# A two-block transformer kernel: when GpSimd sums squares and makes modulation products, and how the first FFN gets its input

## The chip, the cores and the metric

The kernel runs on one core of one Trainium2 chip. The metric is the device time of one launch in microseconds (us). Five engines have instruction streams of their own: TensorE (PE in the profile, with its weight loads as PEld), VectorE (DVE), ScalarE (ACT), GpSimd (POOL) and SyncE (SP), which here only starts DMAs.

## The reference, cut to what matters

Two transformer blocks are applied to x, 512 tokens by 1024 features, in float32. The part of the first block that this case is about, with `mod` a vector of 6 x 1024 modulation values computed from c:

```python
mod = silu(c) @ w_ada + b_ada
sh1, sc1, gt1, sh2, sc2, gt2 = split(mod, 6)
...
x = x + gt1 * (concat(y_a, y_b, y_c) @ w_out)
h = rmsnorm(x, g_ffn) * (1 + sc2) + sh2
gate, up = split(h @ w_gate_up, 2)             # 1024 -> 2 x 2816
x = x + gt2 * ((silu(gate) * up) @ w_down)     # 2816 -> 1024
```

`rmsnorm(x, g)` divides each token by the root of the mean of its 1024 squares plus 1e-6. After it come a final norm and a second block with two more FFNs of the same size.

## The kernel before, in words

**Layout.** Features lie on the 128 partitions and the 512 tokens along the free dimension. x is 8 tiles of 128x512 (`KD` = 8), an FFN's hidden layer 22 such tiles (`KF` = 22). A float32 product is made from three matmuls (`three`, lines 489 to 491): each operand is split into a high part, rounded to the type fp32r by a copy on ScalarE, and a low part, the difference, by a subtraction on VectorE. high x high, high x low and low x high are summed in one PSUM bank.

**Slabs.** Weights come in slabs of 8 tiles (128x1024, 512 KB), one slab for each output tile of 128 features. Slab s uses buffer s % 2 of `w_raw`, `w_hi` and `w_lo`. SyncE loads it once the low part of slab s - 2 is made. `split_high(s)` (line 997, ScalarE, recorded at L1003) waits for the load and for `w_used` of slab s - 2, that is until TensorE is through with that buffer. `split_low(s)` (line 1400, VectorE, recorded at L1404) then makes the low part and counts up `w_ready`, which TensorE awaits. Slabs 20 to 27 are w_out. Slab 28 is the gate slab of pair 0 of the first FFN, 29 its up slab, 30 and 31 those of pair 1, and so on to 71. A pair is one gate slab and one up slab, 24 matmuls each, and gives one hidden tile.

**Order.** Each engine has its own hand-written instruction stream, and semaphores tie them together. `plan` fixes which PSUM bank each product uses and whose reading frees it.

**From the output projection to the FFN.** For each of the 8 output tiles VectorE adds gt1 times the PSUM bank to x (`add_gated`, L1512), ScalarE squares the new tile into `sq` (L1147, two buffers by turns), and GpSimd adds the square to `acc` (`sums("out1", None)`, L1899). When all 8 are in, TensorE sums `acc` over the partitions in `token_sums` (4 matmuls with one column each, recorded as 8 at L692). ScalarE takes the root (`root`, L1180), VectorE the reciprocal (`token_scale`, L1537), and TensorE spreads the 512 reciprocals over all partitions into a PSUM bank (`spread`, L701, again recorded as 8).

**h.** For each tile k VectorE multiplies x by that bank into `x_scaled` (L1552). ScalarE makes from it `h_full` and `h_hi` by one activation each (L1189), both with the factor `scale2` and the shift sh2 for each feature, and VectorE makes `h_lo` = `h_full` - `h_hi` (`low`, L1410). `x_scaled` and `h_full` have two buffers. TensorE waits for `h_lo` of tile k before the three matmuls with it.

**The first FFN.** TensorE's `pair(0)` runs all of gate slab 28 and then all of up slab 29. ScalarE's `pair(n)` is: high part of slab 2n + 1 of the FFN, silu of the gate bank (L1201), high part of slab 2n + 2, then `hid_hi` (L1209). VectorE's is: low part of slab 2n + 1, low part of slab 2n + 2, `t_hid` = up bank times silu (L1572), then `hid_lo` (L1576).

**GpSimd's products.** The six parts of `mod` are computed in the gaps. GpSimd's share for a part j is `mod_products(j)`: for 8 blocks of w_ada (128x1024, loaded on its own DMA queue by `mod_row` into `sq`) a multiplication by c (L1820 or L1822) and an addition into `acc` (L1824). gt2's follow right behind the square sums and the reading of `acc` by TensorE. TensorE reads them in `mod_columns` after the last gate and up pair. `acc` and `sq` are the same memory for squares and products. The next use of `acc` is `sums("down0", ...)`, in the down projection.

Of the kernel before, what the change touches and what calls it, by code (L numbers as in the profile page):

```python
# [25 lines left out]
P = 128  # L26
T = 512
# [96 lines left out]
def program(nc, ins, out):  # L124
    ctx = ExitStack()
    with ctx:
# [75 lines left out]
        (x_scaled, h_full), _ = region(OVER + 3 * T * BYTES, BIG, [(n, [P, 2, T], F32) for n in ("x_scaled", "h_full")])  # L202
# [268 lines left out]
        def _(pe):  # L471
# [233 lines left out]
            token_sums("ffn0", "out1")  # L705
            spread(("scale", "ffn0"), 4, 1)

            def ffn(f, between):
# [21 lines left out]
                pair(0)  # L730
# [252 lines left out]
        def _(act):  # L983
# [197 lines left out]

            root("ffn0")
            act.wait_ge(mod_set, 2)
            for k in range(KD):
                act.wait_ge(scaled_x, k + 1)
                if k >= 2:
                    act.wait_ge(h_ready, 8 * GEN["ffn0"] + k - 1)
                for dst, done_ in ((h_full[:, k % 2, :], h_whole), (h_hi[:, k, :], h_high)):
                    act.activation(dst, x_scaled[:, k % 2, :], ACT.Identity, bias=modc[:, SH2 + k:SH2 + k + 1],  # L1189
                                   scale=scale2[:, k:k + 1]).then_inc(done_, 1)  # L1190

            def ffn(f, between, down, last=False):
                s0 = S_GU[f]

                def pair(n, i=None):
                    split_high(s0 + 2 * n + 1, i, 2)
# [136 lines left out]
        def _(dve):  # L1333
# [210 lines left out]

            token_scale("ffn0")
            b = wait_filled(dve, ("scale", "ffn0"))
            dve.wait_ge(mod_set, 2)
            for k in range(KD + 1):
                if k < KD:
                    if k >= 2:  # L1550
                        dve.wait_ge(h_high, 8 * GEN["ffn0"] + k - 1)
                    dve.tensor_tensor(x_scaled[:, k % 2, :], x[:, k, :], psum[:, b, :], ALU.mult).then_inc(scaled_x, 1)  # L1552
                if k:
                    j = k - 1
                    dve.wait_ge(h_whole, j + 1)
                    low(h_lo[:, j, :], h_full[:, j % 2, :], h_hi[:, j, :], 8 * GEN["ffn0"] + j)

            def ffn(f, between, before_down, down, last=False):
                s0 = S_GU[f]

                def pair(n, i=None):
                    split_low(s0 + 2 * n + 1, i, 2)
# [233 lines left out]
        def _(pool):  # L1796
# [89 lines left out]
            def sums(phase, clear, kinds=1):  # L1886

                if clear:
                    wait_filled(pool, ("sum", clear))
                    done(pool.memset(acc[:, 0:kinds, :], 0.0))  # L1890
                else:
                    pool.memset(acc[:, 0:kinds, :], 0.0).then_inc(summed, SUM0)
                    pool.wait_ge(summed, SUM0)
# [9 lines left out]
            sums("out1", None)  # L1903
            mod_row(GT2 // KD, 0)
            wait_filled(pool, ("sum", "ffn0"))
            mod_products(GT2 // KD)
            wait_filled(pool, ("mod", GT2 // KD))
            sums("down0", "ffn0", 2)
# [55 lines left out]
```

## Time and profile before

| what | value |
|---|---|
| median of 3 timed runs | 1907.98 us (1907.70 to 1912.42) |
| span of the profiled execution | 1908.4 us |
| mean granted TensorE clock | 0.978 |
| busy: TensorE, weight loads | 96%, 75% |
| busy: VectorE, ScalarE, GpSimd | 50%, 35%, 15% |
| DMA traffic | 181.54 MB, mean 95 GB/s |

The page gives no time of the profiled execution beyond its span from the first to the last instruction; it lies 0.4 us from the median. The busy share of TensorE comes from modelled ends of its matmuls, so two matmuls that follow each other overlap in the records; the distance of their starts is what one costs.

### The profile page before, as it was taken

What the parts mean: (1) busy time and instruction counts of PE and PEld (TensorE: products, weight loads), DVE (VectorE), ACT (ScalarE), POOL (GpSimd) and SP (SyncE); (2) the same over time, 40 slices, a digit from 0 to 9 for tenths busy, and PEclk for the clock granted to TensorE, in tenths of its full rate; (3) what the DMA queues carried; (4) which work ended last, traced back from release to release, by engine and by line L of the source; (5) the groups of instructions that cost most, each with busy time, mean ns of one, the idle gap of its engine ahead of it and who ended that gap; (6) DMA issues with size and microseconds to landing.
All of it is one profiled execution on the core that took longest, in us unless ns stands there. A gap on an engine that the chain in (4) does not pass through costs nothing.

```text
span 1908.4 us, 23358 instructions
## 1 busy us (share of the span) xinstructions
PE 1822.8 (96%) x8239; PEld 1435.6 (75%) x8239; DVE 950.1 (50%) x1401; ACT 663.2 (35%) x1048; POOL 290.9 (15%) x208
## 2 busy tenths in 40 slices
PE   5699989699999999999999999999999999999998
PEld 2567667488888887888888887766678888888886
DVE  5689883643333333444434436776655544444322
ACT  2345563322222323222222223554444332222222
POOL 6287511710000111000001010002100100000000
PEclk9799999699999999999999999999999999999999
DMA  9343202433334232333343342112123333333332
GB/s 343 102 137 106 78 23 66 125 96 99 99 89 115 78 98 72 99 94 93 99 120 91 87 102 72 39 54 63 53 73 96 96 88 99 99 95 96 106 93 73
DMA packets 298399, 181.54 MB, mean 95 GB/s; under 512 B 14636, under 2 KB 285416, under 8 KB 298280
## 3 DMA queue, kind: packets, MB, share of 16 engines
q1 hardware_dynamic: 290336, 157.30, 28.1%
q0 software_dynamic: 6352, 22.26, 3.9%
q10 hardware_dynamic: 1656, 1.25, 0.2%
q8 instruction: 34, 0.56, 0.1%
q14 instruction: 21, 0.17, 0.0%
HBM read 178.69 MB, written 3.09 MB: 95 GB/s over the span
## 4 chain that ended last, share of the span: by engine, by line
PE 79%; issue 5%; DVE 2%; POOL 1%; ACT 0%; POOLq 0%; DVEq 0%; ACTq 0%
PE psum L489 25%; PE psum L491 25%; PE psum L490 24%; PE psum L809 3%; PE psum L817 1%; DVE h_lo L1410 1%; POOL acc L1899 1%; PE psum L701 0%; DVE w_lo L1404 0%; PE psum L692 0%; PE psum L780 0%; DVE x_scaled L1552 0%; PE psum L880 0%; DVE o_tok L1791 0%; PE psum L558 0%
## 5 line engine op out<-in xcount | busy, mean ns | idle before, releaser
L489 PE MATMUL psum<-h_hi,w_hi 128*128 128x512 f32 x1480 | 594.0, 401 | 20.1 <-DVE h_lo L1410 11.0
L490 PE MATMUL psum<-h_lo,w_hi 128*128 128x512 f32 x1480 | 580.0, 392 | 0.0
L491 PE MATMUL psum<-h_hi,w_lo 128*128 128x512 f32 x1480 | 580.0, 392 | 0.0
L1404 DVE TENSOR_TENSOR w_lo<-w_raw,w_hi 128x1024 fp32r<-128x1024 f32 (+1 forms) x258 | 366.9, 1422 | 315.9 <-ACT w_hi L1003 312.3
L489 PEld LDWEIGHTS psum<-h_hi,w_hi 128*128 128x128 f32 x1480 | 279.5, 189 | 144.7 <-issue 65.1
L1003 ACT ACTIVATE w_hi<-w_raw 128x1024 fp32r<-128x1024 f32 (+1 forms) x258 | 286.0, 1108 | 154.1 <-PE psum L491 154.0
L491 PEld LDWEIGHTS psum<-h_hi,w_lo 128*128 128x128 f32 x1480 | 279.8, 189 | 59.9
L490 PEld LDWEIGHTS psum<-h_lo,w_hi 128*128 128x128 f32 x1480 | 280.1, 189 | 55.0 <-issue 0.7
L491 PE MATMUL psum<-hid_hi,w_lo 128*128 128x512 f32 x528 | 210.7, 399 | 0.0
L490 PE MATMUL psum<-hid_lo,w_hi 128*128 128x512 f32 x528 | 208.1, 394 | 0.0
L489 PE MATMUL psum<-hid_hi,w_hi 128*128 128x512 f32 x528 | 207.1, 392 | 0.0
L1899 POOL TENSOR_TENSOR acc<-acc,sq 128x512 f32<-128x512 f32 x48 | 66.0, 1374 | 807.7 <-ACT sq L1147 806.8
L1209 ACT ACTIVATE hid_hi<-t_hid 128x512 f32 (+1 forms) x66 | 41.9, 635 | 284.3 <-DVE t_hid L1572 284.3
L490 PEld LDWEIGHTS psum<-hid_lo,w_hi 128*128 128x128 f32 x528 | 99.1, 188 | 25.7
L489 PEld LDWEIGHTS psum<-hid_hi,w_hi 128*128 128x128 f32 x528 | 99.1, 188 | 23.7
L1572 DVE TENSOR_TENSOR t_hid<-psum,t_silu 128x512 f32<-128x512 f32 x66 | 45.7, 692 | 143.0 <-PE psum L491 143.0
L491 PEld LDWEIGHTS psum<-hid_hi,w_lo 128*128 128x128 f32 x528 | 99.1, 188 | 22.8
L1205 ACT ACTIVATE t_silu<-t_gate 128x512 f32<-128x512 f32 x44 | 27.8, 632 | 160.2 <-DVE t_gate L1567 160.2
L1576 DVE TENSOR_TENSOR hid_lo<-t_hid,hid_hi 128x512 f32 (+1 forms) x66 | 46.9, 711 | 64.8 <-ACT hid_hi L1209 64.8
L1824 POOL TENSOR_TENSOR acc<-acc,sq 128x1024 f32<-128x1024 f32 x28 | 75.6, 2700 | 2.2
L1293 ACT ACTIVATE p<-p,stat 128x512 f32<-128x512 f32 (+2 forms) x64 | 41.3, 645 | 83.5 <-DVE stat L1702 43.8
L1120 ACT ACTIVATE p<-p,stat 128x512 f32<-128x512 f32 x64 | 45.8, 717 | 62.2 <-DVE stat L1463 62.2
(247 smaller groups left out, 1936.1 us busy)
## 6 DMA issues: line engine op xcount, KB each, us to landing
w_raw<-in_w_in SPq DMA_DIRECT2D x50, 512.0 KB, 3.8
w_raw<-in_w_gate_up SPq DMA_DIRECT2D x44, 512.0 KB, 3.8
w_raw<-in_ffn_w_gate SPq DMA_DIRECT2D x44, 512.0 KB, 3.9
w_raw<-in_ffn_w_up SPq DMA_DIRECT2D x44, 512.0 KB, 3.8
w_raw<-in_ffn_w_down SPq DMA_DIRECT2D x32, 704.0 KB, 4.5
sq<-in_w_ada POOLq DMA_DIRECT2D x32, 512.0 KB, 4.2
w_raw<-in_w_down SPq DMA_DIRECT2D x16, 704.0 KB, 4.5
ada_w<-in_w_ada SPq DMA_DIRECT2D x4, 2048.0 KB, 20.8
```

Of the source, the lines that this page charges most:

```text
L489: pe.matmul(o, a_hi, b_hi, start=start, stop=False)
L490: pe.matmul(o, a_hi, b_lo, start=False, stop=False)
L491: return pe.matmul(o, a_lo, b_hi, start=False, stop=stop)
L809: pe.matmul(psum[:, b, 0:P * len(kts)], q_, k_, start=True, stop=True).then_inc(filled[b], 1)
L1003: act.activation(w_hi[:, s % 2, 0:n], w_raw[:, s % 2, 0:n], ACT.Identity).then_inc(w_high, 1)
L1120: act.activation(p1[:, t % 3, m, :], p1[:, t % 3, m, :], ACT.Exp, bias=stat[:, t % 3, m:m + 1], scale=-1.0, accum_out=stat[:, t % 3, 2 + m ...
L1209: act.activation(hid_hi[:, slot_of(n, i), :], t_hid[:, :], ACT.Identity).then_inc(hid_high, 1)
L1404: dve.tensor_tensor(w_lo[:, s % 2, 0:n], w_raw[:, s % 2, 0:n], w_hi[:, s % 2, 0:n].bitcast(F32), ALU.subtract).then_inc(w_ready, 1)
L1572: dve.tensor_tensor(t_hid[:, :], psum[:, b, :], t_silu[:, :], ALU.mult).then_inc(hid_set, 1)
L1576: dve.tensor_tensor(hid_lo[:, at, :], t_hid[:, :], hid_hi[:, at, :].bitcast(F32), ALU.subtract)\
L1824: last = pool.tensor_tensor(mod_acc, mod_acc, ada_row[:, k % 2, :], ALU.add)
L1899: pool.tensor_tensor(acc[:, m, :], acc[:, m, :], sq[:, n, m, :], ALU.add).then_inc(summed, 1)
```

## The change

In the stretch between the output projection and the first FFN:

- GpSimd sums only the squares of tiles 0 to 6. TensorE takes the token sums in two groups of 4 matmuls, the first from `acc`, the second directly from the last square, both into the same bank.
- GpSimd's products for gt2 start when two hidden tiles of the first FFN are ready (`hid_ready` 2), no longer right behind the square sums.
- `x_scaled` is made by one VectorE instruction with `scale2` as its factor for each feature and has four buffers. `h_full` is gone: ScalarE makes only `h_hi` (shift alone), and VectorE makes `h_lo` from `x_scaled`, the shift and `h_hi` in one instruction.
- Both parts of slab 29 are split before the root and the reciprocal on ScalarE and VectorE.
- TensorE runs the first gate and up slab of the first FFN together, tile by tile: for each k three matmuls of gate, then three of up.

```diff
@@ memory
-        (x_scaled, h_full), _ = region(OVER + 3 * T * BYTES, BIG, [(n, [P, 2, T], F32) for n in ("x_scaled", "h_full")])
+        (x_scaled,), _ = region(OVER + 3 * T * BYTES, BIG, [("x_scaled", [P, 4, T], F32)])
@@ TensorE
-            token_sums("ffn0", "out1")
+            b = take(("sum", "ffn0"))
+            for part_, ready in ((acc[:, 0, :], (summed, SUM0 + KD - 1)), (sq[:, 1, 0, :], (squared, KD))):
+                pe.wait_ge(*ready)
+                for i in range(TT):
+                    last = pe.matmul(psum[:, b, i:i + 1], part_[:, P * i:P * i + P], mean_d,
+                                     start=ready[0] is summed and i == 0, stop=ready[0] is squared, skip_group_check=True)
+            last.then_inc(filled[b], 1)
             spread(("scale", "ffn0"), 4, 1)
...
-                pair(0)
+                def first_pair():
+                    for n, key in enumerate(("gate", "up")):
+                        await_slab(s0 + n)
+                        take((key, 0, 0))
+                    for k in range(KD):
+                        pe.wait_ge(h_ready, h0 + k + 1)
+                        for n, key in enumerate(("gate", "up")):
+                            last = three(psum[:, bank_of((key, 0, 0)), :], *tile(s0 + n, k), *hs[k], k == 0, k == KD - 1)
+                            if k == KD - 1:
+                                last.then_inc(w_used, 1)
+
+                if f == 0:
+                    first_pair()
+                else:
+                    pair(0)
@@ ScalarE
+            split_high(S_GU[0] + 1)
             root("ffn0")
             act.wait_ge(mod_set, 2)
             for k in range(KD):
                 act.wait_ge(scaled_x, k + 1)
-                if k >= 2:
-                    act.wait_ge(h_ready, 8 * GEN["ffn0"] + k - 1)
-                for dst, done_ in ((h_full[:, k % 2, :], h_whole), (h_hi[:, k, :], h_high)):
-                    act.activation(dst, x_scaled[:, k % 2, :], ACT.Identity, bias=modc[:, SH2 + k:SH2 + k + 1],
-                                   scale=scale2[:, k:k + 1]).then_inc(done_, 1)
+                act.activation(h_hi[:, k, :], x_scaled[:, k % 4, :], ACT.Identity, bias=modc[:, SH2 + k:SH2 + k + 1])\
+                   .then_inc(h_high, 1)
...
-                    split_high(s0 + 2 * n + 1, i, 2)
+                    if f or n:
+                        split_high(s0 + 2 * n + 1, i, 2)
@@ VectorE
+            split_low(S_GU[0] + 1)
             token_scale("ffn0")
+            dve.wait_ge(mod_set, 2)
             b = wait_filled(dve, ("scale", "ffn0"))
-            dve.wait_ge(mod_set, 2)
             for k in range(KD + 1):
                 if k < KD:
-                    if k >= 2:
-                        dve.wait_ge(h_high, 8 * GEN["ffn0"] + k - 1)
-                    dve.tensor_tensor(x_scaled[:, k % 2, :], x[:, k, :], psum[:, b, :], ALU.mult).then_inc(scaled_x, 1)
+                    if k >= 4:
+                        dve.wait_ge(h_ready, 8 * GEN["ffn0"] + k - 3)
+                    dve.scalar_tensor_tensor(out=x_scaled[:, k % 4, :], in0=x[:, k, :], scalar=scale2[:, k:k + 1],
+                                             in1=psum[:, b, :], op0=ALU.mult, op1=ALU.mult).then_inc(scaled_x, 1)
                 if k:
                     j = k - 1
-                    dve.wait_ge(h_whole, j + 1)
-                    low(h_lo[:, j, :], h_full[:, j % 2, :], h_hi[:, j, :], 8 * GEN["ffn0"] + j)
+                    dve.wait_ge(scaled_x, j + 1)
+                    dve.wait_ge(h_high, 8 * GEN["ffn0"] + j + 1)
+                    dve.scalar_tensor_tensor(out=h_lo[:, j, :], in0=x_scaled[:, j % 4, :],
+                                             scalar=modc[:, SH2 + j:SH2 + j + 1], in1=h_hi[:, j, :].bitcast(F32),
+                                             op0=ALU.add, op1=ALU.subtract).then_inc(h_ready, 1)
...
-                    split_low(s0 + 2 * n + 1, i, 2)
+                    if f or n:
+                        split_low(s0 + 2 * n + 1, i, 2)
@@ GpSimd (in sums, the branch without clear)
-                    pool.memset(acc[:, 0:kinds, :], 0.0).then_inc(summed, SUM0)
-                    pool.wait_ge(summed, SUM0)
+                    pool.memset(acc[:, 0:kinds, :], 0.0).then_inc(summed, 1)
+                    pool.wait_ge(summed, SUM0 + SQUARES[phase])
...
-            sums("out1", None)
+            pool.memset(acc[:, 0, :], 0.0).then_inc(summed, SUM0)
+            pool.wait_ge(summed, SUM0)
+            for n in range(KD - 1):
+                pool.wait_ge(squared, n + 1)
+                pool.tensor_tensor(acc[:, 0, :], acc[:, 0, :], sq[:, n % 2, 0, :], ALU.add).then_inc(summed, 1)
+                pool.wait_ge(summed, SUM0 + n + 1)
+            pool.wait_ge(hid_ready, 2)
             mod_row(GT2 // KD, 0)
-            wait_filled(pool, ("sum", "ffn0"))
             mod_products(GT2 // KD)
             wait_filled(pool, ("mod", GT2 // KD))
-            sums("down0", "ffn0", 2)
+            sums("down0", None, 2)
```

## Rows read from the trace of the kernel before

**Rows 1.** The page, part 1: busy time, share of the span, instructions

```profile
PE 1822.8 (96%) x8239; PEld 1435.6 (75%) x8239; DVE 950.1 (50%) x1401; ACT 663.2 (35%) x1048; POOL 290.9 (15%) x208
```

**Rows 2.** Timeline of TensorE: start us, us, engine, line, operation, count [idle before <-releaser]

```profile
344.20 1.87 PE L692 MATMUL psum<-small,acc 128*128 128x1 f32 x8 [3.08 <-POOL acc L1899]
346.63 2.08 PE L701 MATMUL psum<-ident,rcol 128*128 128x128 f32 x8 [0.57 <-DVE rcol L1537]
351.99 0.77 PE L489 MATMUL psum<-h_hi,w_hi 128*128 128x512 f32 x1 [3.28 <-DVE h_lo L1410]
...
374.26 0.80 PE L489 MATMUL psum<-h_hi,w_hi 128*128 128x512 f32 x1 [1.65 <-DVE w_lo L1404]
...
388.01 0.50 PE L489 MATMUL psum<-h_hi,w_hi 128*128 128x512 f32 x1 [0.94 <-DVE w_lo L1404]
```

**Rows 3.** The chain that ended last, single matmuls: start us, us, what

```profile
375.05 0.43 PE psum L490
...
378.65 0.23 PE psum L491
```

**Rows 4.** Stretches: length, busy us of PE, PEld, DVE, ACT, POOL, PEclk, DMA share, GB/s

```profile
306.00:308.00 2.00, 0.72 (x4) 0.26 (x2) 1.46 (x2) 0.44 (x1) 0.86 (x1) 1.00 0.00 0
...
343.00:344.00 1.00, 0.00 (x0) 0.00 (x0) 0.00 (x0) 0.00 (x0) 1.00 (x1) 0.80 0.15 43
...
368.00:372.00 4.00, 2.69 (x6) 1.66 (x6) 4.00 (x3) 1.71 (x2) 3.91 (x3) 0.50 0.42 131
...
377.00:378.00 1.00, 1.00 (x4) 0.83 (x3) 0.04 (x1) 0.00 (x0) 1.00 (x1) 0.64 1.03 311
```

**Rows 5.** Timeline of ScalarE from the last square on

```profile
342.18 0.63 ACT L1147 ACTIVATE sq<-x_res 128x512 f32 x1 [3.78 <-DVE x_res L1512]
...
349.53 0.81 ACT L1189 ACTIVATE h_full<-x_scaled,modc,scale 128x512 f32<-128x512 f32 x1 [3.16 <-DVE x_scaled L1552]
...
372.64 0.60 ACT L1201 ACTIVATE t_silu<-psum 128x512 f32<-128x512 f32 x1 [2.92 <-PE psum L491]
373.14 1.05 ACT L1003 ACTIVATE w_hi<-w_raw 128x1024 fp32r<-128x1024 f32 x1
```

**Rows 6.** Timeline of VectorE: y stage, scale, first FFN pair

```profile
299.49 0.75 DVE L1495 SCALAR_TENSOR_TENSOR k<-o,sub,psum 128x512 f32<-128x512 f32 x1 [0.27 <-PE psum L664]
300.15 0.69 DVE L1410 TENSOR_TENSOR h_lo<-k,h_hi 128x512 fp32r<-128x512 f32 x1
300.76 0.74 DVE L1495 SCALAR_TENSOR_TENSOR k<-o,sub,psum 128x512 f32<-128x512 f32 x1
...
348.74 1.28 DVE L1552 TENSOR_TENSOR x_scaled<-x_res,psum 128x512 f32<-128x512 f32 x2 [2.17 <-PE psum L701]
...
381.73 0.69 DVE L1572 TENSOR_TENSOR t_hid<-psum,t_silu 128x512 f32<-128x512 f32 x1 [4.70 <-PE psum L491]
383.20 1.92 DVE L1576 TENSOR_TENSOR hid_lo<-t_hid,hid_hi 128x512 fp32r<-128x512 f32 x1 [0.77 <-ACT hid_hi L1209]
385.04 2.91 DVE L1404 TENSOR_TENSOR w_lo<-w_raw,w_hi 128x1024 fp32r<-128x1024 f32 x1
```

**Rows 7.** The line that subtracts for h_lo: durations ns min/median/max

```profile
L1410 DVE TENSOR_TENSOR h_lo<-h_full,h_hi x8: 693/2264/2881, 351.1 to 368.0; 128x512 fp32r<-128x512 f32 x8
```

**Rows 8.** Timeline of GpSimd: last square sum, first and last product

```profile
342.88 1.26 POOL L1899 TENSOR_TENSOR acc<-acc,sq 128x512 f32<-128x512 f32 x1 [4.05 <-ACT sq L1147]
...
348.90 1.89 POOL L1820 TENSOR_TENSOR acc<-sq,cact 128x1024 f32<-128x1024 f32 x1 [2.00 <-DMA sq<-in_w_ada]
...
386.95 3.26 POOL L1824 TENSOR_TENSOR acc<-acc,sq 128x1024 f32<-128x1024 f32 x1
```

**Rows 9.** Groups by line: kinds of row nearest to the new operations

```profile
L1404 DVE TENSOR_TENSOR w_lo<-w_raw,w_hi 128x1024 fp32r<-128x1024 f32 (+1 forms) x40 | 49.8, 1246 | 67.5 <-ACT w_hi L1003 66.4
...
L1158 ACT ACTIVATE h_hi<-x_res,vcol x12 | 8.7, 724 | 68.3 <-DVE x_res L1627 48.3 <-DVE x_res L1778 20.0
...
L1521 DVE SCALAR_TENSOR_TENSOR h_lo<-x_res,vcol,h_hi x14 | 10.5, 752 | 15.4 <-ACT h_hi L1158 15.4
```

## The prediction, made before the changed kernel ran

> **What bounds the kernel now.** I read the page first. TensorE is busy 96% of the span and no other engine over half of it [rows 1], so only time in which TensorE waits or runs slowly can be gained. The 40 slices put such time ahead of about 400 us. The timeline of TensorE then shows the stretch of this change. Its last out-projection matmul ends at about 341.1 (344.20 less 3.08 of idling). The token sums start at 344.20, the spread at 346.63, the first FFN matmul at 351.99, the up slab only at 374.26, and up slab 31 waits until 388.01 [rows 2]. When TensorE doesn't wait, one matmul follows the next after 0.43 us at the lower clock and 0.23 us (24 in 5.44 us) at the higher one [rows 3]. The stretches tell which clock it was: the granted clock halves (2.4 to 1.2 GHz) at about 343.6, some 2.5 us after TensorE went idle, stays at 0.50 through the whole gate slab, where TensorE is busy 2.7 of 4 us, and is back at full at about 377.7, after some 3.4 us of matmuls without a wait [rows 4]. The gate slab took 20.6 us (351.99 until silu, which its end releases, at 372.64 [rows 5]). At full clock it would be 5.44 us.
>
> Why it took so long is in VectorE's and GpSimd's rows. A subtraction of two SBUF tiles, 128x512, takes 0.69 us in the y stage [rows 6], but the eight of `h_lo` have a median of 2.26 and a maximum of 2.88 us [rows 7]. In just this stretch GpSimd runs its products, 348.90 to 390.21 [rows 8]. `x_scaled`, which reads one operand from PSUM, is not drawn out beside them: two in 1.28 us [rows 6]. So VectorE's instructions with two SBUF tiles share something with GpSimd, and they pace TensorE.
>
> **The change, part by part** (times in us on the profiled execution's axis).
>
> **Square sums in two groups.** Now: square done at 342.81 [rows 5], GpSimd's addition 1.26 us [rows 8], token sums from 344.20 to 346.07 [rows 2]. The first group has its input early and runs at about 341.2 behind the last matmul. The second can start at 342.85; if it costs as much as all of today's (1.87 at the lower clock) it ends at 344.7, and the root would let VectorE go on at 345.0. But slab 29's split now stands in front: high part on ScalarE right behind the square, 342.72 plus 1.05 [rows 5], low part on VectorE from 343.8 for 1.25 to 1.45 us (1.25 is the mean of 40 in the FFN [rows 9]). The reciprocal therefore comes at about 345.2. Behind it as now 0.2 us for itself and 2.08 for the spread [rows 2]: `x_scaled` starts at 347.5 where it is 348.74 [rows 6]. **Gain 1.2**. Bounds: 0.8 (a w_lo of 1.5 and a slower second group) and 2.3 (the clock hasn't fallen yet, and the spread takes half). The split itself costs nothing, as until here both engines wait; without that cover it would be 2.3 us, as now after `h`.
>
> **h from x.** To the first `h_lo` now 3.25 us: `x_scaled`, two activations, subtraction [rows 2, 5, 6]. After: an instruction of the kind with a PSUM operand 0.75 [rows 6], one activation with one column of factors or shifts 0.72, a scalar_tensor_tensor of two SBUF tiles 0.75 [rows 9], and 0.25 for three handovers: 2.5 us, first matmul at 350.0. **Gain 0.75**. From then VectorE makes one `h_lo` every 1.33 us: 0.66 from start to start after the kind with PSUM [rows 6], and by its length some 0.67 for the other. ScalarE needs 0.7 for each and isn't the bound. The last is ready at about 359.2.
>
> Here a rule speaks against the change. The rows have the new kind, 0.752 us for 128x512 with x and `h_hi` both in SBUF [rows 9], next to 0.69 for the plain subtraction. The Trainium skill, Vector Engine (DVE) Microarchitecture Reference, section 7 (Points that are easy to get wrong), says that a scalar_tensor_tensor with two SBUF sources that aren't bf16 runs at half throughput. By it one `h_lo` would cost about 1.4 us and the pace be 2.0; by the row the sum stays as it is. I take the row.
>
> **Gate and up together.** TensorE has 48 matmuls, six for each tile: 2.56 us at the lower clock, 1.36 at the higher. Both are more than 1.33, so once started it doesn't wait. The clock is low at 350.0, as TensorE did only small work for 9 us. It rose 3.4 us after the last wait before 377.7 [rows 2, 4]; I take 3.4 to 6.8 and 5.1 as the middle: 12 matmuls slow, 36 at 0.227 = 8.2, up slab done at 363.3 (now 381.7). From start to end that is 13.3 us where it is 29.7. **Gain 16.4**. Bounds: 15.5 and 18.8 (clock high throughout).
>
> **A new wait.** Slab 30 needs slab 28's buffer. Until now that was split under up slab 29; now both buffers come free together. Gate's last matmul ends 0.7 us before up's, at 362.6. Then silu 0.50 to the next start, high part 1.05 [rows 5], low part 1.25 to 1.4: gate slab 30 starts at 365.65 instead of right behind slab 29. **Loss 2.4**. Behind that chain on VectorE is `t_hid`, on ScalarE `hid_hi` and the high part of 31: 0.7 + 0.7 + 1.05 + 1.4 and a `hid_lo` beside it bring slab 31 by 369.6, before slab 30 is through at 371.1. So today's wait of 1.1 us in front of slab 31 (slab 30 is through at 381.5 + 5.44 = 386.9, slab 31 starts at 388.01 [rows 2]) goes. **Gain 1.1**. Slab 31 then starts at 371.1 where it is 388.0: 16.9 so far (the terms add to 17.0).
>
> **The products, later.** They cost the same 41.3 us of GpSimd [rows 8], now from some 2.5 us (the load) after the second hidden tile, over 3 to 4 pairs of 10.9 us. Their result is awaited only after all 22 pairs, some 200 us later; their 8 loads of 512 KB (4 MB in 41 us, 100 GB/s) come beside the kernel's mean of 95 GB/s, where the first slices of the page moved 343. What they do to VectorE is in the rows: in the pair under them `t_hid` at 381.73, `hid_lo` 1.92 us, w_lo 2.91 us, TensorE at 388.01 [rows 2, 6]. That chain, 6.3 us after the up slab, is longer than the 5.44 of the gate slab beside it, hence a wait of 0.94. If only one of the two is drawn out (1.23 or 1.66 less) it fits and nothing is lost. Bounds: 0, and 4 pairs at 2.3, the chain with the longest 2.88 [rows 7] and a w_lo of 3.3. I take half of the measured 0.94 in 3.5 pairs, as only some of GpSimd's instructions will meet each of the two. **Loss 1.8**.
>
> **Sum**: 1.2 + 0.75 + 16.4 - 2.4 + 1.1 - 1.8 = 15.2; by the absolute times 15.1. The profiled span is 0.4 us above the median 1907.98, so I subtract from the median: 1892.9, call it 1893. Everything behind slab 31 moves by the same amount, as TensorE has no other wait up to the down projection.
>
> **The rivals.**
>
> **The clock stays low (8%).** If the clock doesn't rise during the joint pair, its 48 matmuls take 20.5 us instead of 13.3: 7.2 us less, **1900**. For it: it stayed at 0.50 for 22 us in the gate slab. Against: there TensorE waited in front of each tile [rows 4], and it rose as soon as it didn't.
>
> **It falls again in the new wait (10%).** 2.4 us of idling is nearly the 2.5 after which it fell at 343.6; in 306 to 308 TensorE was busy 0.72 of 2 us and it held [rows 4]. Slab 30 would then run 3.4 us at half speed, costing 1.7: **1894.7**.
>
> **Half throughput of the new `h_lo` (4%).** If the new subtraction takes twice the plain one's 0.69, VectorE makes one tile in 0.66 + 1.38 = 2.0 us [rows 6]; the last is ready at 350.0 + 7 x 2.0 = 364.0, and its six matmuls end at 365.5 instead of 363.3: 2.2 us less, **1895**. Against: the 0.752 us of fourteen such instructions [rows 9].
> That is what the cited page of the Trainium skill would give; the trace of before doesn't agree with it.
>
> **Slower: the products hold VectorE for their whole length (3%).** Place: `hid_lo` and w_lo of slabs 2n + 1 in the pairs under the products. If each waits for one full product (5.6 us, an eighth of 41.3 and its DMA issue) the chain is 0.7 + 0.7 + 5.6 + 5.6 = 12.7, 7.3 more than the gate slab, in 3.5 pairs 25 us: **1916**. It decides from a wait of 16.9 / 3.5 = 4.8 us for each pair on. Against: no `h_lo` took more than 2.9 us under the same products [rows 7]. A milder form of it, 3 to 4 us for each pair, would end within 0.3%.
>
> **How the numbers follow.** The forecast has 72%, the rivals 25%, the rest is for what I don't see. A change under 0.3% (5.7 us) can't be told from none here. Faster by more hold the forecast, the low clock, the fall in the wait and the halved `h_lo`, less what could go wrong with each: 0.93. Within: 0.04. Slower: 0.03. Range: upwards the kind of loss the products can bring (up to 9) less some chance, and a late clock: 1899. Downwards a clock that holds or rises early (2.4), an earlier spread (1) and no loss by the products (1.8), not all together: 1889.
>
> **What would show it.** Right: eight `h_lo` at 0.75 us, 1.33 apart; the first FFN matmul at about 350; one rise of the clock between 353 and 357; up slab done at 363, then a wait of 2.4 us released by w_lo; three or four waits under 1 us in front of up slabs while GpSimd works, from about 385 to 430; none behind. The forecast is wrong if `h_lo` is 1.4 us long, if the clock is at 0.50 behind 357, or if the waits in the pairs under the products are over 2 us each.

## The result and the profile after

The changed kernel takes 1894.88 us (median of 4 runs, 1893.66 to 1897.02) where the one before takes 1910.20 (4 runs beside them; 1907.98 was the median of three of these). The ratio is 0.9921, 95% interval 0.9908 to 0.9935. Forecast were 1893 and a range of 1889 to 1899. The profiled execution has a span of 1895.2 us and took 1897.02, the slowest of the four. In every execution the time is 1.7 to 1.9 us more than the span. One execution of the kernel before, beside a later group of runs, took 2089.43 us at a mean granted clock of 0.823 and counts in no number here.

The page has the same work in less time. TensorE's busy time is 6.6 us less and VectorE's 5.3; ScalarE lost its eight `h_full` instructions and GpSimd one addition:

```profile
PE 1816.2 (96%) x8247; PEld 1436.2 (76%) x8247; DVE 944.8 (50%) x1401; ACT 656.8 (35%) x1040; POOL 291.1 (15%) x207
```

Where the time went is in the timeline of TensorE, from the token sums on:

```profile
338.39 0.95 PE L709 MATMUL psum<-small,acc 128*128 128x1 f32 x8
340.30 1.43 PE L709 MATMUL psum<-small,sq 128*128 128x1 f32 x8 [0.96 <-ACT sq L1167]
342.60 2.08 PE L701 MATMUL psum<-ident,rcol 128*128 128x128 f32 x8 [0.86 <-DVE rcol L1556]
347.36 0.77 PE L489 MATMUL psum<-h_hi,w_hi 128*128 128x512 f32 x1 [2.68 <-DVE h_lo L1578]
...
362.45 0.50 PE L489 MATMUL psum<-h_hi,w_hi 128*128 128x512 f32 x1 [2.21 <-DVE w_lo L1423]
...
391.82 0.64 PE L489 MATMUL psum<-h_hi,w_hi 128*128 128x512 f32 x1 [1.85 <-DVE w_lo L1423]
...
406.05 0.50 PE L489 MATMUL psum<-h_hi,w_hi 128*128 128x512 f32 x1 [1.44 <-DVE w_lo L1423]
...
417.83 0.50 PE L489 MATMUL psum<-h_hi,w_hi 128*128 128x512 f32 x1 [0.59 <-DVE w_lo L1423]
...
597.48 1.84 PE L558 MATMUL psum<-small,acc 128*128 128x1 f32 x16
```

These answer to [rows 2]. The last row is the first column sum for gt2, behind the 22 pairs; in the kernel before it stands at

```profile
611.18 1.84 PE L558 MATMUL psum<-small,acc 128*128 128x1 f32 x16
```

Absolute times need care here. The last square starts at 339.62 us in this profile (342.18 before, [rows 5]), and that lies ahead of everything the change touches. I therefore measure all steps from the start of the last square. To the gt2 columns it is 269.0 us before and 257.9 after: 11.1 us gained in the stretch, 2.6 ahead of it.

The stretches (columns as in [rows 4]) show the granted clock: it rises 3.7 us after the first FFN matmul, holds in the new wait behind the joint pair, and falls once more behind the wait that ends at 391.82:

```profile
351.00:352.00 1.00, 1.00 (x6) 0.83 (x5) 1.00 (x3) 0.40 (x2) 0.00 (x0) 0.97 0.00 0
...
360.00:362.00 2.00, 0.24 (x2) 0.00 (x0) 0.83 (x1) 1.13 (x2) 0.00 (x0) 1.00 0.00 0
...
392.00:395.00 3.00, 3.00 (x8) 2.32 (x9) 3.00 (x1) 0.00 (x0) 2.69 (x3) 0.50 0.56 168
395.00:396.00 1.00, 1.00 (x5) 0.81 (x4) 0.08 (x1) 0.00 (x0) 1.00 (x1) 0.79 0.55 74
```

On VectorE the eight `h_lo` take 0.75 us, as against a median of 2.26 [rows 7]. The lengthening has moved: below are a low part that starts just behind GpSimd's first product, then `hid_lo` and the two low parts behind it in the first whole pair under the products (6.74 us for the two), and a low part in the next pair. Without products a low part takes 1.23 us and `hid_lo` 0.69.

```profile
L1578 DVE SCALAR_TENSOR_TENSOR h_lo<-x_scaled,modc,h_hi x8: 743/746/752, 346.5 to 355.3; 128x512 fp32r<-128x512 f32 x8
```

```profile
380.70 2.93 DVE L1423 TENSOR_TENSOR w_lo<-w_raw,w_hi 128x1024 fp32r<-128x1024 f32 x1 [3.28 <-ACT w_hi L1023]
...
386.33 2.09 DVE L1601 TENSOR_TENSOR hid_lo<-t_hid,hid_hi 128x512 f32 x1 [1.01 <-ACT hid_hi L1228]
388.34 6.74 DVE L1423 TENSOR_TENSOR w_lo<-w_raw,w_hi 128x1024 fp32r<-128x1024 f32 x2
...
402.58 3.41 DVE L1423 TENSOR_TENSOR w_lo<-w_raw,w_hi 128x1024 fp32r<-128x1024 f32 x1
```

GpSimd's products run from 380.66 to 422.86, 42.2 us where it was 41.3:

```profile
380.66 1.89 POOL L1845 TENSOR_TENSOR acc<-sq,cact 128x1024 f32<-128x1024 f32 x1 [2.85 <-DMA sq<-in_w_ada]
...
419.61 3.25 POOL L1849 TENSOR_TENSOR acc<-acc,sq 128x1024 f32<-128x1024 f32 x1
```

### The profile page after: what moved, and what is told of

Read it like the earlier page. It is cut to its first block, busy times and chain, and to the rows that moved or that the text cites. A ratio compares the mean times of both kernels' runs of the same rounds, so it can differ in the third digit from the quotient of the medians.

```text
span 1895.2 us, 23342 instructions
## 1 busy us (share of the span) xinstructions
PE 1816.2 (96%) x8247; PEld 1436.2 (76%) x8247; DVE 944.8 (50%) x1401; ACT 656.8 (35%) x1040; POOL 291.1 (15%) x207
## 4 chain that ended last, share of the span: by engine, by line
PE 88%; DVE 7%; issue 2%; DMA 1%; ACT 1%; ACTq 0%; DVEq 0%; SPq 0%
PE psum L489 28%; PE psum L491 27%; PE psum L490 27%; PE psum L829 3%; DVE w_lo L1423 2%; PE psum L837 1%; DVE first_acc L1397 1%; DVE p L1492 1%; DVE p L1482 1%; DMA ada_w<-in_w_ada 1%; PE psum L607 1%; ACT w_hi L1023 1%; DVE wt_lo L1500 0%; PE psum L701 0%; PE psum L558 0%
## 5 line engine op out<-in xcount | busy, mean ns | idle before, releaser
L1423 DVE TENSOR_TENSOR w_lo<-w_raw,w_hi 128x1024 fp32r<-128x1024 f32 (+1 forms) x258 | 371.1, 1439 | 319.3 <-ACT w_hi L1023 315.9
L1925 POOL TENSOR_TENSOR acc<-acc,sq 128x512 f32<-128x512 f32 x40 | 55.6, 1391 | 723.5 <-ACT sq L1167 722.5
L1601 DVE TENSOR_TENSOR hid_lo<-t_hid,hid_hi 128x512 f32 (+1 forms) x66 | 48.3, 731 | 64.8 <-ACT hid_hi L1228 64.8
L1312 ACT ACTIVATE p<-p,stat 128x512 f32<-128x512 f32 (+2 forms) x64 | 41.3, 645 | 83.2 <-DVE stat L1727 43.5
```

The costliest lines, as they stand in the source:

```text
L1423: dve.tensor_tensor(w_lo[:, s % 2, 0:n], w_raw[:, s % 2, 0:n], w_hi[:, s % 2, 0:n].bitcast(F32), ALU.subtract).then_inc(w_ready, 1)
L1601: dve.tensor_tensor(hid_lo[:, at, :], t_hid[:, :], hid_hi[:, at, :].bitcast(F32), ALU.subtract)\
L1925: pool.tensor_tensor(acc[:, m, :], acc[:, m, :], sq[:, n, m, :], ALU.add).then_inc(summed, 1)
```

## The experiments

All times below are from one profile of each kernel and count from the start of its last square. "First matmul" is the first of the FFN, "gate" the time from there to silu, "gt2" the start of the gt2 column sums. The waits are the idle times that the profile shows; where the clock holds, each costs 0.2 to 0.3 us more than its idle time by the starts of the matmuls, as the last matmul before it and the first behind it take longer. The ratio is that of the whole time to the kernel before, run on the same chip.

| kernel | first matmul | gate | wait before slab 30 | waits before up slabs | gt2 | ratio, 95% interval |
|---|---|---|---|---|---|---|
| before | 9.81 | 20.65 | none | 0.94 | 269.0 | 1 |
| changed | 7.74 | 12.23 | 2.21 | 1.85, 1.44, 0.59 | 257.9 | 0.9921 (0.9908 to 0.9935) |
| changed, again | 7.73 | 12.35 | 2.21 | 0.46, 0.59, 0.57 | 254.5 | 0.9927 (0.9913 to 0.9940) |
| e1 only late products | 8.84 | 11.93 | none | 0.47, 0.61, 0.57 | 257.8 | 0.9948 (0.9934 to 0.9961) |
| e2 products early | 9.18 | 20.52 | 4.09 | none | 264.7 | 0.9982 (0.9973 to 0.9991) |
| e3 gate, then up | 7.15 | 9.78 | none | 0.47, 0.61, 0.57 | 253.6 | 0.9929 (0.9915 to 0.9943) |
| e4 one product | 7.73 | 12.23 | 2.21 | none | 251.4 | 0.9915 (0.9900 to 0.9929) |
| e5 one group | 9.27 | 13.17 | 2.21 | 0.47, 0.61, 0.59 | 258.4 | 0.9944 (0.9930 to 0.9958) |
| e6 h_full again | 8.33 | 12.10 | 2.21 | 1.87, 0.30, 0.26 | 255.3 | 0.9945 (0.9932 to 0.9959) |
| e7 paced products | 7.73 | 12.26 | 2.21 | none | 251.5 | 0.9905 (0.9892 to 0.9919) |
| e8 joint to tile 3 | 7.25 | 9.91 | 0.18 | 0.46, 0.60, 0.56 | 251.6 | 0.9908 (0.9894 to 0.9923) |
| e9 paced, joint to 3 | 7.32 | 9.88 | 0.16 | none | 248.7 | 0.9903 (0.9886 to 0.9920) |
| e9's kernel again (e12) | 7.73 | 10.15 | 0.18 | none | 249.4 | 0.9892 (0.9875 to 0.9908) |
| e10 paced, gate then up | 7.73 | 9.79 | none | none | 251.3 | 0.9916 (0.9901 to 0.9931) |

Whole times scatter by 2 to 9 us for each kernel, 5 us as a rule, the one before included (spans of 1905 to 1911), and the profiles show where most of it comes from: the last square starts between 338.5 and 339.8 us in some and at 342 to 345 in others, and the mean granted clock between 100 and 340 us is 0.99 in the first kind and 0.95 to 0.97 in the second. That stretch is the attention of the first block; no edit touches it. So the column "gt2" tells the parts apart, not the ratio. The clock's rise also falls at different points, which moves single steps by some 0.5 us.

**e1: only the products later**, in the kernel before.

```diff
-            mod_row(GT2 // KD, 0)
             wait_filled(pool, ("sum", "ffn0"))
+            pool.wait_ge(hid_ready, 2)
+            mod_row(GT2 // KD, 0)
             mod_products(GT2 // KD)
```

> The kernel before with one edit: gt2's products on GpSimd start at hid_ready 2, everything else as before. My theory (the parts need each other): h_lo falls from 2.3 to 0.7 us, but the two activations for each tile on ScalarE then set the pace at about 1.45 us, slab 29 is still split only behind h, and the products cost about 6 us in the later pairs; it saves 2 to 6 us against before. Rival (moving the products is nearly the whole gain): it saves 11 us or more.

The rival was nearly right: 11.2 us in the stretch, 10.2 by the medians. Set against the 14.5 us of the changed kernel's second profile, this one edit is some three quarters. (1.0 of the 11.2 is the first matmul, which comes earlier only because the clock was still high in the token sums: 1.05 us for them, 1.87 in [rows 2].) `h_lo` is back at its own length:

```profile
L1410 DVE TENSOR_TENSOR h_lo<-h_full,h_hi x8: 686/693/694, 353.1 to 363.7; 128x512 fp32r<-128x512 f32 x8
```

ScalarE's two activations set the pace, as expected, but at 1.42 to 1.5 us a tile that is nearly the pace of gate's matmuls at the lower clock, so gate ends 11.9 us after its start instead of 20.7. What I had overrated is all else. Against the changed kernel again, the longer chain to the first matmul costs 1.1 us and the pair 2.3 (slab 30 starts 17.5 us after the first matmul, not 15.2); the products cost 2.8 us of waits and not 6.

**e2: the changed kernel with the products early.**

```diff
-            pool.wait_ge(hid_ready, 2)
             mod_row(GT2 // KD, 0)
+            wait_filled(pool, ("sum", "ffn0"))
             mod_products(GT2 // KD)
```

> The changed kernel with the products back right behind the token sums. My theory: x_scaled and h_lo alternate at about 2.9 us a tile again, the six matmuls of a tile (2.56 us at the lower clock) wait for each, the joint pair ends about 25 us after its start instead of 13, no wait in the later pairs but one: it saves 3 to 7 us against before. Rival (the joint pair is what gains, the move of the products only adds waits of 6 us): it saves 16 us or more.

4.3 us in the stretch, 3.2 by the medians: my theory, not the rival. The pair itself was mis-sized: up ends 21.2 us after the first matmul, not 25, and 4.09 us of waiting for slab 30 follow. Behind that wait the clock falls too, for 3.5 us. The new `h_lo` is drawn out as much as the old, and `x_scaled`, with one operand in PSUM, isn't:

```profile
L1578 DVE SCALAR_TENSOR_TENSOR h_lo<-x_scaled,modc,h_hi x8: 2197/2226/2870, 351.5 to 370.4; 128x512 fp32r<-128x512 f32 x8
```
```profile
L1572 DVE SCALAR_TENSOR_TENSOR x_scaled<-x_res,scale,psum x8: 733/735/747, 349.8 to 367.6; 128x512 f32<-128x512 f32 x8
```

Joint or not, the pair can't be faster than `h_lo`: 20.5 us to silu as before. Together, e1 and e2 give 11.2 + 4.3 = 15.5, near the whole 14.5: the products' move is some three quarters of the gain (11.2 alone, 10.2 on top of the others), the other edits the rest.

**e3: gate slab whole, then up.**

```diff
-                if f == 0:
-                    first_pair()
-                else:
-                    pair(0)
+                pair(0)
```

> The changed kernel, but the first gate slab runs whole before the up slab. My theory: VectorE makes a tile in 1.32 us and a gate tile takes 1.28 us at the lower clock, so gate ends about 11.5 us after its start, up follows in 5.4 to 8 us, and slab 30 has no wait of 2.4 us before it: 2 to 4 us slower than the changed kernel, that is 11 to 13 us saved. Rival (the joint pair carries the 16 us of that step of the prediction): under 5 us saved.

In the stretch my theory missed in the good direction (the medians differ by 12.0 us, within it): 253.6 instead of 254.5, 0.9 us less than the changed kernel, 0.6 of which is an earlier clock ahead of the first matmul. Slab 30 starts 15.1 us after the first matmul in e3, and 15.1 and 15.2 in the changed kernel. The joint pair gives nothing. What it saves by six matmuls for each `h_lo` it pays in the wait of 2.2 us before slab 30.

**e4: one product.** Seven of the eight blocks of w_ada for gt2 are left out, load and arithmetic.

```diff
-            mod_products(GT2 // KD)
+            rows_loaded[0] += 16
+            pool.wait_ge(row_landed[0], rows_loaded[0])
+            pool.tensor_tensor(mod_acc, ada_row[:, 0, :], cact[:, 0:1].to_broadcast([P, D]), ALU.mult).then_inc(mod_summed, 1)
+            pool.wait_ge(mod_summed, GT2 // KD - 1)
```

> The changed kernel with only the first of the eight products of gt2 (seven blocks of w_ada and their multiplications and additions are left out). My theory: the three waits of 2.0, 1.6 and 0.8 us in front of up slabs and the 3.4 us at the lower clock go: 6 us below the changed kernel, 21 saved against before. Rival (the lower clock there is not due to the wait): 4.4 us below the changed kernel.

All three waits are gone and with them the fall of the clock: 6.4 us less than the changed kernel's first profile, as expected. But by the medians it saved 15.0 us against the kernel before, not 21, and the ratio was hardly below the changed kernel's, so I looked again.

**The changed kernel again**, without an edit.

> The changed kernel once more, since leaving out seven products (e4) saved 6.5 us between the token sums and the gt2 columns in the profile but under 1 us in the mean of the runs. My theory: the waits under the products vary little, so from the first token sum to the gt2 columns it again takes about 259 us, and what differs between runs lies ahead of the change, in the attention stage, where the profiles differ by 5 us already: first token sum between 338 and 344 us. Rival (the products' loss depends on how they fall against the pairs): 253 to 257 us, with waits in front of up slabs under 2 us in sum.

The rival was right: 255.7 us from the first token sum (254.5 from the last square), with waits of 0.46, 0.59 and 0.57 us. TensorE's rows:

```profile
390.48 0.50 PE L489 MATMUL psum<-h_hi,w_hi 128*128 128x512 f32 x1 [0.46 <-DVE w_lo L1423]
402.26 0.51 PE L489 MATMUL psum<-h_hi,w_hi 128*128 128x512 f32 x1 [0.59 <-DVE w_lo L1423]
414.05 0.50 PE L489 MATMUL psum<-h_hi,w_hi 128*128 128x512 f32 x1 [0.57 <-DVE w_lo L1423]
```

VectorE's and GpSimd's tell why. Here `hid_lo` (L1601) slips through between two GpSimd instructions at its own length, and only the low part (L1423) is long; in the first profile both were. It starts just as GpSimd's multiplication (L1847) ends:

```profile
386.38 0.71 DVE L1601 TENSOR_TENSOR hid_lo<-t_hid,hid_hi 128x512 f32 x1 [1.01 <-ACT hid_hi L1228]
387.12 3.30 DVE L1423 TENSOR_TENSOR w_lo<-w_raw,w_hi 128x1024 fp32r<-128x1024 f32 x1
```
```profile
384.63 1.91 POOL L1847 TENSOR_TENSOR sq<-sq,cact 128x1024 f32<-128x1024 f32 x1
386.62 2.73 POOL L1849 TENSOR_TENSOR acc<-acc,sq 128x1024 f32<-128x1024 f32 x1
```

Against e4 the products cost 3.1 us here and 6.4 in the first profile. The starts of TensorE's matmuls show 2.7 and 6.3 of it in front of up slabs and right behind; here a fourth small delay of 0.3 us (up slab 41) adds to the three waits. Four other profiles with late products that aren't paced (e1, e3, e5, e8) have the same waits as here, to 0.03 us; e6 began with 1.87, like the first profile.

Which of the two happens goes with who starts first when the first product meets a low part. In this profile:

```profile
380.75 1.23 DVE L1423 TENSOR_TENSOR w_lo<-w_raw,w_hi 128x1024 fp32r<-128x1024 f32 x1 [3.28 <-ACT w_hi L1023]
```
```profile
380.98 2.75 POOL L1845 TENSOR_TENSOR acc<-sq,cact 128x1024 f32<-128x1024 f32 x1 [3.12 <-DMA sq<-in_w_ada]
```

VectorE is 0.23 us ahead and keeps its 1.23 us, and GpSimd's multiplication takes 2.75 where it takes 1.89 alone. In the first profile GpSimd is 0.04 us ahead (380.66 and 380.70): it keeps 1.89, and the low part takes 2.93. Both times the second ends 1.1 to 1.8 us after the first, nearly its own whole length. Of the seven unpaced profiles of late products, the low part starts first in five (by 0.10 to 0.49 us), all with a first wait of 0.46 to 0.47; GpSimd starts first in two (by 0.04 and by 0.01 us in e6), and they have 1.85 and 1.87. The next product then starts 2.8 us (first profile) or 3.9 us (here) after that low part did. No run moved that start on purpose.

**e5: one group of token sums.**

```diff
-            for part_, ready in ((acc[:, 0, :], (summed, SUM0 + KD - 1)), (sq[:, 1, 0, :], (squared, KD))):
...
+            token_sums("ffn0", "out1")
...
-            for n in range(KD - 1):
+            for n in range(KD):
                 pool.wait_ge(squared, n + 1)
```

> The changed kernel with all 8 squares summed on GpSimd and one group of token sums. My theory: slab 29's split (low part until about 0.15 us before the reciprocal in the changed kernel) hides part of what the two groups gain; the chain is 1.3 us longer at GpSimd, so 0.8 to 1.3 us slower between the last square and the first FFN matmul than the changed kernel's 7.74 us. Rival (the groups gain nothing as the split sets the time): under 0.3 us.

The first matmul comes 1.5 us later (9.27 against 7.73), a little over the upper end. This profile also shows the forecast's second rival happen: behind the wait of 2.21 us the clock falls for 3.4 us (columns as in [rows 4]).

```profile
363.00:364.00 1.00, 0.22 (x1) 0.22 (x2) 1.00 (x2) 0.00 (x0) 0.00 (x0) 0.85 0.00 0
364.00:367.00 3.00, 3.00 (x8) 2.32 (x9) 2.04 (x3) 1.58 (x2) 0.00 (x0) 0.50 0.59 168
367.00:368.00 1.00, 1.00 (x6) 0.82 (x5) 0.20 (x1) 0.00 (x0) 0.00 (x0) 0.94 0.07 20
```

In the other profiles with a wait of 2.21 us (changed, again, e4, e6, e7) the clock held. Of the 3.9 us that e5 loses against 254.5, 1.5 is the first matmul, 0.8 a later rise of the clock in the pair, and the rest this fall.

**e6: h by way of h_full**, all else as in the changed kernel.

```diff
-                act.activation(h_hi[:, k, :], x_scaled[:, k % 4, :], ACT.Identity, bias=modc[:, SH2 + k:SH2 + k + 1])\
-                   .then_inc(h_high, 1)
+                if k >= 2:
+                    act.wait_ge(h_ready, 8 * GEN["ffn0"] + k - 1)
+                for dst, done_ in ((h_full[:, k % 2, :], h_whole), (h_hi[:, k, :], h_high)):
...
```

> The changed kernel with h as before: x_scaled without the factor and two buffers, h_full and h_hi by two activations, h_lo as their difference. My theory: ScalarE's two activations (0.70 from start to start each) set the pace at 1.4 us a tile and the two buffers tie it to h_lo; e1 showed 1.42 to 1.5. At 1.5 the six matmuls of a joint tile (1.36 at the higher clock) wait a little in the last tiles: first FFN matmul 0.7 us later than the changed kernel's 7.73 after the last square, and 1 to 2 us more from the last square to the gt2 columns than a1's 254.5. Rival (h from x is a large part of the gain, as its step in the old kernel had 2.8 us a tile): over 5 us more.

Close to what I expected: the first matmul 0.6 us later, the pair no longer, and 0.8 us more to gt2 where I had 1 to 2. The waits in front of the up slabs differ again (1.87, then 0.30 and 0.26), so gt2's 255.3 can't be set against 254.5 to the tenth; the 0.6 can. Making h straight from x is worth that much in this profile. The ratio is 0.0018 to 0.0024 above the changed kernel's, 3.4 to 4.6 us. But four of e6's five executions have a mean clock of at most 0.982, and the profiled one, the fastest, 0.986; so the medians don't settle what the step is worth.

**e7: the products in step with the pairs.** GpSimd waits until VectorE has just finished a low part, and starts each instruction in the gap behind it. Only the first multiplication isn't timed so: the low part that it asks for is made before its row has landed.

```diff
+                    s = S_GU[0] + 2 * k + 5
+                    pool.wait_ge(w_ready, s + 1)
...
                         done(pool.tensor_tensor(ada_row[:, k % 2, :], ada_row[:, k % 2, :],
                                                 cact[:, k:k + 1].to_broadcast([P, D]), ALU.mult))
+                        pool.wait_ge(w_ready, s + 2)
                         last = pool.tensor_tensor(mod_acc, mod_acc, ada_row[:, k % 2, :], ALU.add)
```

> The changed kernel with gt2's products in step with the pairs: each multiplication waits until the low part of an up slab is made, each addition until that of the next gate slab, one product for each of eight pairs. My theory: VectorE's hid_lo and the up slab's low part then meet no GpSimd instruction, no wait in front of up slabs over 0.2 us and no fall of the clock there; the stretch from the first token sum to the gt2 columns as in e4, about 253 us. Rival (the DMA of w_ada beside the slabs' loads is part of the loss): waits remain, over 2 us in sum.

251.5, as without the products (e4), and no wait. The loads of w_ada are all there, though over twice the time, so this run alone doesn't clear them. The rows of the changed kernel again do: its low part ends at 390.42, 0.06 us before TensorE goes on, and is 2.07 us longer than alone, against a wait of 0.46; it waited for no load. The meeting of GpSimd's and VectorE's instructions explains the loss.

**e8: joint only for tiles 0 to 3**, then gate's tiles 4 to 7, then up's.

```diff
-                    for k in range(KD):
-                        pe.wait_ge(h_ready, h0 + k + 1)
-                        for n, key in enumerate(("gate", "up")):
+                    order = [(k, n) for k in range(4) for n in range(2)]
+                    order += [(k, n) for n in range(2) for k in range(4, KD)]
+                    for k, n in order:
+                        if n == 0:
+                            pe.wait_ge(h_ready, h0 + k + 1)
...
```

> The changed kernel with gate and up together for tiles 0 to 3 only, then gate's tiles 4 to 7, then up's. My theory: gate ends 2.7 us ahead of up instead of 0.7, so the high and low parts of slab 30 lie beside it and the wait of 2.4 us before slab 30 shrinks to about 0.4: 2.0 us less from the first FFN matmul (after 15.1 now) to slab 30. Rival (gate's tiles 4 to 7 outrun VectorE's h_lo): a wait of over 1 us for h_lo in the pair.

The wait before slab 30 shrinks from 2.21 to 0.18 and none for `h_lo` comes in: 251.6, 2.9 us less than 254.5: 0.5 by the first matmul and 2.4 from there to slab 30, of which 2.0 is the wait.

**e9, e12 and e10: the two together, and pacing without the joint pair.** e9 is e7 plus e8; e10 is e7 plus e3.

> The changed kernel with the products in step with the pairs (e7) and the joint pair for tiles 0 to 3 only (e8). My theory: the two gains add, as they lie in different places: 3.0 and 2.0 to 2.9 us from a1's 254.5, so 249 us from the last square to the gt2 columns, no wait in front of an up slab; the time 5 us under the changed kernel's. Rival (the wait before slab 30 comes back in front of slab 31, as hid_hi and the next split still hang on the up slab): 251 us.

> The changed kernel with the products in step with the pairs and gate slab 28 whole before up slab 29. My theory: e3's 253.6 less the 3 us of its three waits, so 250.5 from the last square to the gt2 columns, between e7's 251.5 and e9's: the joint pair by itself is worth nothing, since VectorE's 1.32 us for a tile is about what a gate tile takes at the lower clock and the pair has no wait of 2.4 us behind it. Rival (e3 was low only since its clock rose early): 253 us or more.

> e9's kernel once more, because whole times scatter by 5 us from the attention stage ahead of the change, and e9's ratio of 0.9903 overlaps that of the changed kernel (0.9921, again 0.9927). My theory: from the last square to the gt2 columns again 248.7 us, within 0.5, and a ratio of 0.989 to 0.991. Rival (the stretch's gain is lost elsewhere in the program): a ratio over 0.992 with the same stretch.

e9 gives 248.7 as expected, e12 249.4, 0.7 more and outside the 0.5 that I had allowed; 0.4 of that is the first matmul and 0.3 the pair, both by when the clock was high, and nothing is lost behind them. By the medians e9 is only 1.4 and 2.6 us under the changed kernel's two, where I had 5; e12 is 5.7 and 6.9 under them. e10's 251.3 is 0.8 above my 250.5, about what e3 had gained by its earlier clock: the joint pair in the changed kernel is still worth nothing (e7 has 251.5), the half-joint one 1.9 to 2.6. In e12 VectorE and GpSimd interlock without touching from the second product on (the first meets a low part and takes 2.82 us; in e9 it starts first and the low part takes 2.91, without a wait of TensorE behind it):

```profile
384.40 0.69 DVE L1604 TENSOR_TENSOR hid_lo<-t_hid,hid_hi 128x512 f32 x1 [1.01 <-ACT hid_hi L1231]
385.14 1.23 DVE L1426 TENSOR_TENSOR w_lo<-w_raw,w_hi 128x1024 fp32r<-128x1024 f32 x1
...
389.65 1.23 DVE L1426 TENSOR_TENSOR w_lo<-w_raw,w_hi 128x1024 fp32r<-128x1024 f32 x1 [3.28 <-ACT w_hi L1026]
```
```profile
386.52 1.89 POOL L1852 TENSOR_TENSOR sq<-sq,cact 128x1024 f32<-128x1024 f32 x1 [3.89 <-DVE w_lo L1426]
391.02 2.40 POOL L1855 TENSOR_TENSOR acc<-acc,sq 128x1024 f32<-128x1024 f32 x1 [2.61 <-DVE w_lo L1426]
```

VectorE's low part ends at 386.37, GpSimd multiplies from 386.52 to 388.41; the next ends at 390.88, GpSimd adds from 391.02. This version is the best of those tried by the stretch: 5.1 to 5.8 us under the changed kernel's 254.5. By the ratios alone it is less clear: 0.9892 (0.9875 to 0.9908) for e12 just touches the changed kernel's 0.9908 to 0.9935, and 0.9903 (0.9886 to 0.9920) for e9 overlaps it. What differs is mostly the attention stage: all four executions of e12 have a mean clock of at least 0.984, of e9's only one. Those five took 1888.35 to 1890.17 us; the changed kernel's seven with such a clock took 1893.66 to 1897.02.

## Why the prediction was right

The time, 1894.88, was forecast to 0.1% (1893). Most of the missing 1.9 us is in the base and not in a step: the span of 1908.4 was held against the median 1907.98, but an execution takes 1.8 us more than its span, so the profiled one took about 1910.2, which is also the later median. By its steps, from the last square on, before and after:

- **Two groups of sums**: `x_scaled` starts 5.17 us after the square where it was 6.56, 1.4 gained (forecast 1.2). e5, without it, has 6.71, so it is worth 1.5. Right, and as foreseen the second group wasn't the last to be awaited: the low part of slab 29 was.
- **h from x**: 3.25 becomes 2.57, 0.7 gained (0.75). One `h_lo` every 1.32 us (1.33). The rule of the Trainium skill (Vector Engine (DVE) Microarchitecture Reference, section 7) that a scalar_tensor_tensor with two SBUF sources that aren't bf16 has half the throughput doesn't show: 0.746 us for 512 columns, against 0.69 for the plain subtraction.
- **Gate and up together**: 12.9 us from the first matmul to the end of up (forecast 13.3, before 29.7). The size was right; the name was wrong. The prediction booked 16.4 us under this heading, 14.0 with the new wait taken off. Slab 30 starts 29.5 us after the first matmul before the change, 15.1 and 15.2 in the changed kernel's two profiles and 15.1 in e3, so the joint order gives none of it; in e1, by the freed `h_lo` alone, it is 17.5, so that gives 12.0 of 14.4. The prediction never priced the order against gate first with the same fast `h_lo`; then it would have seen that 1.28 us for a gate tile at the lower clock and 1.33 for an `h_lo` are the same pace. The clock rose 3.7 us after the start, where 5.1 was taken as the middle of 3.4 to 6.8. No row showed the 6.8; in the joint pairs with undisturbed `h_lo` it rose between 2.9 (e9) and 5.7 us (e5) after it.
- **The new wait**: 2.21 idle, 2.4 from start to start, as forecast. Slab 31 follows without a wait. It starts at 28.4 us instead of 45.8 [rows 2, 5]: 17.4 gained (16.9).
- **The products, later**: here a size was off. Forecast was a loss of 1.8 us, given as half of 0.94 in 3.5 pairs, which is 1.6 (with the 1.1 from start to start it is 1.9). It is 3.1 in the usual case and 6.4 in the first profile (e4 as the measure). The meetings of the two engines are not independent chances: in each of three pairs the low part met a GpSimd instruction for its whole length (3.3 to 3.4 us, where the prediction's row had 2.9), so a wait came every time. In the first profile the clock fell besides, behind a wait of 1.85 us, which the prediction allowed only for the wait behind the joint pair.
- **The rivals**: the clock rose in time in every profile with late products. Its fall behind the joint pair came in one of six profiles with a wait of 2.21 us (e5), near the 10% given. Half throughput of `h_lo` didn't come (its price left out that the first `h_lo` would be 0.6 us later, too). Nor did a VectorE instruction wait for a full product of 5.6 us; but it does wait out nearly the rest of the one GpSimd instruction that it meets, a smaller form of that rival. The longest w_lo was 3.42 us.

The stretch gained 11.1 us in the first profile and 14.5 in the second, forecast 15.1; the medians differ by 15.3. That the last agrees best is in part luck: the scatter ahead of the change is 5 us for each execution. Two of the four executions of the kernel before took 1912.4 to 1912.5 us and two 1907.7 to 1908.0, while all four of the changed kernel have a mean clock of at least 0.984, so its attention stage was probably quick in all of them. And the total hides two misses that cancel in part: slab 31 gained 0.5 us more than forecast, the products lost 1.3 more in the usual case and 4.6 in the first profile.

What stays open is why the attention stage has the lower clock in some executions and not in others. And that the lengthening needs two SBUF tiles on VectorE's side is shown for these instructions only (L1572 with PSUM kept its 0.74 us in e2); no experiment changed a given instruction's operands from one kind to the other. Nor is it shown what decides whether the clock falls behind a given wait.

## What to carry to other kernels

When one engine's instructions are longer in one stretch than the same kind elsewhere, look for the other engine that works just then, and move or pace that work before reordering anything else: here it was some three quarters of the gain. Work that disturbs is best started from the semaphore that ends the disturbed engine's last urgent instruction, so that it fills a known gap. And price a reordering against the plain order with all other edits in, or it gets the credit of its neighbours.

## What the runs showed of the hardware that I had not expected

- A VectorE subtraction of two SBUF tiles of 128x1024 takes 1.23 us alone and up to 3.42 beside GpSimd's additions. GpSimd's instructions are lengthened too: the addition takes 2.39 us alone (e12) and up to 3.27 (e6), the multiplication 1.89, and 2.48 (e1) to 2.93 (e10) when a low part is under way.
- Where GpSimd's first product met a low part, the one that started first kept its length and the other gave way, even at a lead of 0.04 us: 1.89 (GpSimd) and 2.93 us (VectorE) in the changed kernel's first profile, 1.23 (VectorE) and 2.75 us (GpSimd) in its second.
- A wait of 1.85 us on TensorE was once followed by a fall of the granted clock (2.4 to 1.2 GHz, 3.4 us long), while one of 1.87 us (e6) and five of six of 2.21 us passed without. Whether such a wait costs extra can't be told from its length alone.
- The same stretch gave waits of about 0.46, 0.6 and 0.57 us in five profiles, 1.85, 1.44 and 0.59 in one, and 1.87, 0.30 and 0.26 in another (e6): two engines in step can fall into one of a few patterns, and a single profile shows just one.
